# Sample value products of a hybrid decoder step: fp32 in pairs, or split into high and low parts row by row

## What is computed

```python
def attn_sample(q, k_new, v_new, iq, iw, ik_new, cache_k, cache_v, cache_ik, layer,
                page_table, rel_table):
    ...
    idx, valid = indexer_topk(iq, iw, ik_all, q_pos, topk)      # 256 of 1025 keys
    ...
    return sparse_attn(q, select(cache_k, k_new), select(cache_v, v_new), idx, q_pos,
                       valid, rel_table)

def sparse_attn(q, k_sel, v_sel, idx, q_pos, valid, rel_table):
    ...
    p = jax.nn.softmax(logits, axis=-1)
    out = jnp.einsum('btngk,btknd->btngd', p.astype(v_sel.dtype), v_sel)
```

## Time and profile before

| | us |
|---|---|
| median of three runs | 886.94 (886.18 to 889.48) |
| the profiled execution's own time | 886.94 |
| its span in the profile | 884.8 |
| PE busy | 847.3 |
| DVE busy | 581.1 |
| ACT busy | 427.4 |
| GpSimd (POOL) busy | 395.9 |
| sample value products, first and last start | 682.6 and 729.5 |

### The profile page before, as it was taken

One profiled execution on the slowest core, in us unless ns is written; L12 is line 12 of the kernel. 1 busy time (PEld: TensorE's weight loads), 2 busy tenths in 40 slices (PEclk: granted clock), 3 DMA queues, 4 the chain that ended last, 5 costly groups with the idle time before them and its releaser, 6 DMA issues.

```text
span 884.8 us, 18265 instructions
## 1 busy us (share of the span) xinstructions
PE 847.3 (96%) x6501; PEld 781.3 (88%) x6501; DVE 581.1 (66%) x1152; ACT 427.4 (48%) x1221; POOL 395.9 (45%) x575
## 2 busy tenths in 40 slices
PE   3999989999999999999999999898899999999998
PEld 3989979799999999999999999677688759998998
DVE  3536777899988998899956177866755337536111
ACT  5646573244455586584547366555534325422100
POOL 1443645219735583567662453287940205501310
PEclk9999999999999999999999999999899999999999
DMA  8212213101103120322033344833253544342422
GB/s 261 75 38 56 64 30 92 59 1 49 49 1 101 68 92 7 96 73 90 8 107 96 110 131 112 231 102 102 72 142 98 170 142 168 100 123 72 128 85 73
DMA packets 79422, 81.33 MB, mean 92 GB/s; under 512 B 20234, under 2 KB 68026, under 8 KB 79082
## 3 DMA queue, kind: packets, MB, share of 16 engines
q1 hardware_dynamic: 77722, 74.97, 28.3%
q0 software_dynamic: 1616, 5.25, 2.5%
HBM read 62.85 MB, written 17.34 MB: 91 GB/s over the span
## 4 chain that ended last, share of the span: by engine, by line
PE 57%; issue 14%; DMA 8%; DVE 7%; SPq 6%; POOL 4%; ACT 2%; DVEq 0%; POOLq 0%; ACTq 0%
PE psum L2116 16%; PE psum L1247 11%; PE psum L2113 7%; DMA index_keys_T<-in_cache_ikt,index_page_rows 6%; PE psum L1217 5%; SPq L565 4%; DVE flag L1899 3%; PE psum L2012 3%; SPq L556 3%; POOL w_low L514 2%; PE psum L1203 2%; PE psum L1996 2%; PE psum L1317 2%; PE psum L1182 2%; DVE bit_kept L1913 1%
## 5 line engine op out<-in xcount | busy, mean ns | idle before, releaser
L2116 PE MATMUL psum<-w_high,xT_high 128*128 128x256 f32 x720 | 204.2, 284 | 0.1
L2116 PE MATMUL psum<-w_low,xT_high 128*128 128x256 f32 x720 | 201.9, 280 | 0.0
L2116 PE MATMUL psum<-w_high,xT_low 128*128 128x256 f32 x720 | 201.6, 280 | 0.0
L1899 DVE TENSOR_SCALAR_CACHE_REDUCE flag<-scores,candidate 128x384 f16<-128x384 f32 (+2 forms) x192 | 181.7, 946 | 6.8
L514 POOL TENSOR_TENSOR w_low<-w_raw,w_high 128x256 fp32r<-128x256 f32 (+1 forms) x168 | 122.3, 763 | 78.8 <-ACT w_high L1576 69.4
L2116 PEld LDWEIGHTS psum<-w_high,xT_high 128*128 128x128 f32 x720 | 127.4, 177 | 2.6 <-ACT psum L1688 0.3
L2116 PEld LDWEIGHTS psum<-w_low,xT_high 128*128 128x128 f32 x720 | 127.6, 177 | 2.3
L2116 PEld LDWEIGHTS psum<-w_high,xT_low 128*128 128x128 f32 x720 | 127.4, 177 | 2.4
L2113 PE MATMUL psum<-xT_high,w_high 128*128 128x384 f32 (+3 forms) x312 | 102.1, 327 | 1.6 <-DVE xT_low L1826 1.2
L2113 PE MATMUL psum<-xT_high,w_low 128*128 128x384 f32 (+3 forms) x312 | 99.7, 320 | 0.0
L2113 PE MATMUL psum<-xT_low,w_high 128*128 128x384 f32 (+3 forms) x312 | 99.6, 319 | 0.0
(11 more groups left out here) (318 smaller groups left out, 1928.7 us busy)
## 6 DMA issues: line engine op xcount, KB each, us to landing
w_raw<-in_w_main SPq DMA_DIRECT2D x40, 512.0 KB, 3.9
page_keys<-in_cache_kt SPq DMA_DIRECT2D x64, 128.0 KB, 2.6
page_values<-in_cache_v SPq DMA_DIRECT2D x64, 128.0 KB, 2.2
x_rows<-in_x_prompt SPq DMA_DIRECT2D x8, 512.0 KB, 5.8
x_res<-in_x_prompt SPq DMA_DIRECT2D x32, 128.0 KB
out<-y_rows SPq DMA_DIRECT2D x32, 128.0 KB
hgate_spill<-stage SPq DMA_DIRECT2D x16, 128.0 KB
ho_spill<-ho_rows SPq DMA_DIRECT2D x4, 512.0 KB, 3.9
```

The lines of the kernel that those rows point to most:

```text
L1899: dve.tensor_scalar(JK[:, 0:w], sc, threshold(k), None, op, ALU.add, accum_out=CNT[:, k:k + 1]).then_inc(s["dve_chain"], 1)
L2116: last = pe.matmul(ps(BANK[n], w, rows(i)), x[:, k, row0(i):row0(i) + rows(i)], ww[:, sl, k, 0:w], start=first, stop=final)
```

## The change

The value products are made of split operands, and row by row:

- **Operands.** ACT copies each row's 128 x 2048 values to a rounded fp32r tile, page_values_high (two of them, a new job "values_high" two steps ahead of the products). DVE subtracts it from the values and writes page_values_low over the raw tile (a new job "values_low", one step ahead). prob_T is split into high and low as well, when it is copied out of PSUM.
- **Products.** For each page, one fp32r product with 40 stationary columns (8 high probabilities, 24 of other rows whose results are not read, 8 low probabilities) against the high values, and one with the 8 high probabilities against the low values. The product of the two low parts is left out. The new value's product stays fp32. Row b's job does all its pages, with outputs at partitions 0 and 32 of one half of the bank.
- **Outputs.** ACT copies the part at partition 32, and DVE adds the part at partition 0.
- **Buffers.** Three raw buffers take the place of five; the other two hold the high parts. SP loads rows 0 to 2 ahead, and rows 3 to 7 behind the mix loads, each when the products of row b-3 are done. The first output weights wait for seven rows of products and no longer for six.

```diff
-        VP = [over(W0 + o, (f"page_values_{x}", [NPG, UW], F32))[0]
-              for x, o in enumerate((-8192, 0, 16384, 8192, 24576))]
+        VP, VPL = ([over(W0 + o, (f"page_values{part}_{x}", [NPG, UW], dt))[0] for x, o in enumerate((-8192, 0, 16384))]
+                   for part, dt in (("", F32), ("_low", F32R)))
+        VPH = [over(W0 + o, (f"page_values_high_{x}", [NPG, UW], F32R))[0] for x, o in enumerate((8192, 24576))]
...
-        PTP, _e = over(S0 + SCW * 4, ("prob_T", [NPG, BR], F32))
+        PTP, _e = over(S0 + SCW * 4, ("prob_T", [NPG, 2, 2, 32], F32R))
...
-        for n in range(SB):
-            SIDE.setdefault(VALUES_AT[n], []).append(("values", n))
+        for b in range(SB):
+            SIDE.setdefault(VALUES_AT[b] - 2, []).insert(0, ("values_high", b))
+            side = SIDE.setdefault(VALUES_AT[b] - 1, [])
+            side.insert(0 if b > 0 else len(side), ("values_low", b))
+            SIDE.setdefault(VALUES_AT[b], []).append(("values", b))
...
-                x = b % 5
+                x = b % 3
...
-                elif b < 5:
-                    sp.wait_ge(s["sample_hgrn_ready"], 1)
-                    sp.wait_ge(s["sample_state_out"], 32)
                 else:
-                    sp.wait_ge(s["sample_values_done"], 2 if b < 7 else 4)
+                    sp.wait_ge(s["sample_values_done"], b - 2)
...
-            for b in range(5):
+            for b in range(3):
                 load_value_pages(b)
...
-            for b in range(5, SB):
+            for b in range(3, SB):
                 load_value_pages(b)
-            sp.wait_ge(s["sample_values_done"], SB - 2)
+            sp.wait_ge(s["sample_values_done"], SB - 1)
...
-            sp.wait_ge(s["sample_out_copied"], SB // 2)
+            sp.wait_ge(s["sample_out_copied"], 2 * SB)
...
-                elif kind == "values" and b % 2 == 1:
+                elif kind == "values":
                     act.wait_ge(s["sample_values_done"], b + 1)
-                    o = b // 2 % 2 * UW
-                    act.activation(OSM[0:SB, b - 1, :], ps(6, UW, AH, 0, o), ACT.Copy)
-                    act.activation(OSM[0:SB, b, :], ps(6, UW, 32 + AH, 32, o), ACT.Copy).then_inc(s["sample_out_copied"], 1)
+                    act.activation(OSM[0:SB, b, :], ps(6, UW, 32 + SB, 32, b % 2 * UW), ACT.Copy)\
+                        .then_inc(s["sample_out_copied"], 1)
+                elif kind == "values_high":
+                    act.wait_ge(s[f"value_pages_in{b % 3}"], 128 * (b // 3 + 1))
+                    if b < 2:
+                        act.wait_ge(s["sample_hgrn_ready"], 1)
+                        act.wait_ge(s["sample_state_out"], 32)
+                    else:
+                        act.wait_ge(s["sample_values_done"], b - 1)
+                    act.activation(VPH[b % 2][:, :, :], VP[b % 3][:, :, :], ACT.Copy).then_inc(s["sample_values_high"], 1)
...
-                    dve.tensor_copy(PTP[:, :, :].rearrange("p g n -> p (g n)"), ps(6)).then_inc(s["sample_probs_T_ready"], 1)
+                    high, low = PTP[:, :, :, 0, :], PTP[:, :, :, 1, :]
+                    probs = ps(6).rearrange("p (g a n) -> p g a n", g=NPG, a=2)
+                    link(dve.tensor_copy(high, probs))
+                    dve.tensor_tensor(low, probs, f(high), ALU.subtract).then_inc(s["sample_probs_T_ready"], 1)
...
+                elif kind == "values_low":
+                    dve.wait_ge(s["sample_values_high"], b + 1)
+                    dve.tensor_tensor(VPL[b % 3][:, :, :], VP[b % 3][:, :, :], f(VPH[b % 2][:, :, :]), ALU.subtract)\
+                        .then_inc(s["sample_values_low"], 1)
+                elif kind == "values":
+
+                    dve.wait_ge(s["sample_out_copied"], 2 * b + 1)
+                    dve.tensor_tensor(OSM[0:SB, b, :], OSM[0:SB, b, :], ps(6, UW, SB, o=b % 2 * UW), ALU.add)\
+                        .then_inc(s["sample_out_copied"], 1)
...
+                    pe.wait_ge(s["sample_values_low"], b + 1)
...
+                    ge(pe, s["sample_out_copied"], 2 * b)
+                    both, first = ps(6, UW, 32 + AH, o=b % 2 * UW), ps(6, UW, AH, o=b % 2 * UW)
+                    probs = PTP[:, :, :, :, :].rearrange("p g a k n -> p (g a k n)")
+                    for g in range(NPG):
+                        o = 128 * g + 64 * (b // 4) + AH * (b % 4)
+                        if g == NPG - 1:
+                            pe.matmul(first, PN[0:SB, AH * b:AH * (b + 1)], VN[0:SB, :], start=False, stop=False)
+                            pe.matmul(first, probs[:, o:o + AH], VPL[b % 3][:, g, :], start=False, stop=False)
+                        last = pe.matmul(both, probs[:, o:o + 32 + AH], VPH[b % 2][:, g, :], start=g == 0, stop=g == NPG - 1)
+                        if g < NPG - 1:
+                            pe.matmul(first, probs[:, o:o + AH], VPL[b % 3][:, g, :], start=False, stop=False)
```

More of the change, by code:

```diff
@@ L1226, in mix @@
                 if x == 0:
-                    pe.wait_ge(s["sample_out_copied"], SB // 2)
+                    pe.wait_ge(s["sample_out_copied"], 2 * SB)
                 for h in range(2):
@@ L1303, in sample @@
                 elif kind == "values":
-                    pair, half = b // 2, b % 2
-                    first = 2 * pair
-                    if half == 0:
-                        for x in (first, first + 1):
-                            pe.wait_ge(s[f"value_pages_in{x % 5}"], 128 * (x // 5 + 1))
-                        ge(pe, s["sample_out_copied"], pair - 1)
+                    pe.wait_ge(s["sample_values_low"], b + 1)
                     if b == 0:
@@ L1312, in sample @@
                         pe.wait_ge(s["new_prob_ready"], 1)
-                    out_ = [ps(6, UW, 32 * x + AH, 32 * x, pair % 2 * UW) for x in range(2)]
-                    for g in range(4 * half, 4 * half + 4):
-                        for x in range(2):
-                            h = slice(AH * (first + x), AH * (first + x + 1))
-                            last = pe.matmul(out_[x], PTP[:, g, h], VP[(first + x) % 5][:, g, :], start=g == 0, stop=False)
-                    if half == 1:
-                        for x in range(2):
-                            h = slice(AH * (first + x), AH * (first + x + 1))
-                            last = pe.matmul(out_[x], PN[0:SB, h], VN[0:SB, :], start=False, stop=True)
+                    ge(pe, s["sample_out_copied"], 2 * b)
[9 more added lines that the diff above has]
+                            pe.matmul(first, probs[:, o:o + AH], VPL[b % 3][:, g, :], start=False, stop=False)
                     last.then_inc(s["sample_values_done"], 1)
```

## The result

The changed kernel takes 891.1 us (median of 20 runs), the kernel before 883.9 us (20 runs). The ratio is 1.0068, 95% interval 1.0048 to 1.0089: slower by 4 to 8 us, where 5.7 us were forecast (892.6 against 886.94, the median of the first three runs, which lay 3.0 us above that of the twenty). The profiled execution spans 887.0 us. PE is as busy as before, 96%; ACT and DVE have the conversions on top.

The account below looks back on a forecast made before the run. PE, busy 96%, was taken as the bound, waiting on SP's page loads: row 7 lands at 726.7, conversions end 731.5, first mix 737.6 instead of 732.02. So 886.94 + 5.6, with tenths 892.6 us; range 888.0 to 896.0.

Parts of the forecast that it names:

- S: Stretch from the first value product to the first mix transpose, 49.25 us in the kernel before; 5.6 us more forecast.
- The hole before and its cause: Attention loop, after step 33's transposes: PE idle 2.11 us plus 1.52 at low clock, 3.6 us, ended by SP's pace.
- Late rows set the end: Page loads on SP: row 3 first issued at 685.3, periods of 8.8; row 7 lands at 726.7, 4.8 us later.
- Behind the landing: After row 7's pages land at 726.7: conversions and add until 731.5, then DVE's branch to the first mix at 737.6.
- PE's products: Value products: sixteen fp32r records 1.89 us plus new-value product 0.43 per row; eight rows 18.6 us, 1.8 lost while warm.
- Conversions of rows 0 to 6 hidden: ACT copies and DVE subtractions for these rows cost nothing, hidden under PE's scores, attention values and transposes.
- PE's idle time ahead of row 7: Before the last values group: 4 us or more, in two pieces, ended by ACT's exp and DVE's subtraction.
- B: Rival: the same chain with SP never held up, 4.2 us lost, 891.0 us; chance 0.22.
- A: Main case: the sum over late pages and the chain behind row 7's landing, 892.6 us; chance 0.60.
- C: Rival: pages come in time, only PE's own work counts, 20.4 becomes 18.6 us, time 885.1; chance 0.07.
- D: Rival: SP held up in each period, or low clock twice: about 8.5 us, 895.4; chance 0.08.
- E: Rival: split products run at the 0.215 step, not 0.118; 1.6 us more per row, 899 or above; chance 0.03.

Follow-up runs that it names:

- experiment 3: Kernel before, with fixed page numbers in place of the page table's, so no register loads per row: ratio 0.9963 to the kernel before, S = 45.63 us.
- experiment 4: Kernel before, with the loads of mix 0 and 1 issued by GpSimd instead of SP: 882.65 us against 884.96, ratio 0.9967, S = 45.63 us.
- experiment 1: Kernel before, with only rows 3 and 4 loaded behind the mix loads; products, buffers and engines' work unchanged: ratio 1.0057, S = 54.74 us.
- second look: The same changed kernel profiled once more, nothing edited: S = 55.85 us and one time of 892.71 us.
- Experiment 6: Changed kernel with DVE's first two mix_rows at steps 28 and 31 instead of 33: ratio 1.0102 to the kernel before, S = 53.06 us.
- experiment 2: Changed kernel with fixed page numbers in place of the page table's, so no register loads per row: ratio 0.9999 to the kernel before, S = 48.59 us.
- experiment 7: Changed kernel with ACT writing each row's high part twice: ratio 1.0117, S = 61.19 us.
- experiment 8: Changed kernel with mix loads and pages of rows 4 and 6 fetched by GpSimd, first two mix_rows at steps 28 and 31: ratio 1.006, S = 52.62 us.
- experiment 9: Changed kernel with GpSimd's four gating products held back until row 2's high part is there, no DMA on GpSimd: S = 55.59 us in one execution.
- experiment 10: Like experiment 8, but GpSimd makes its four gating products before fetching row 4's pages: ratio 0.999, S = 49.04 us.

## Why the prediction was right

The direction, the size and the mechanism held: S grew by 5.1 and 6.6 us in two profiles where 5.6 were forecast. That the time itself came within 1.5 us of 892.6 is in part luck: the base of 886.94 was 3.0 us above the median of twenty runs, and the loss was somewhat above the sum (7.2 us between the medians). Point by point:

- **The hole before and its cause.** 3.6 us, from SP's pace: shown twice, by taking the register loads away (experiment 3) and by taking the mix loads off SP (experiment 4), with S = 45.63 in both.
- **Late rows set the end.** Shown by experiment 1, in which they alone cost 0.57%. Row 3 first issued 2.6 us behind the first value product in the forecast, 2.9 and 3.9 measured; periods 8.8 in the forecast, 8.82 and 8.98 in the mean; row 7's landing 6.2 us behind its first issue, 6.0 and 5.8 measured.
- **Behind the landing.** Landing to DVE's add: 4.8 us forecast, 4.6 measured. Landing to mix: 10.9 forecast, 10.2 and 10.3 measured. DVE's branch with the two mix_rows ended last in the first profile, as said; in the second look PE's did, the two nearly level. Experiment 6 took the mix_rows away, and PE's branch ended last.
- **PE's products.** Sixteen fp32r records at 0.118 us: right. The new-value product was taken at 0.43 us; its two records stand in the chain with 0.52. A row's job lasts 2.5 us (711.31 to 713.84 in experiment 2), not 2.3, of which the step behind it gives a little back, and the change's own cost with early pages is 3.0 us (experiments 2 and 3), 2.4 of them PE's, and not 1.8. This term was mis-sized, and it did not reach the time because the pages were later still.
- **Conversions of rows 0 to 6 hidden.** Right in the sum; PE's idle time for a low part is 0.37 us once. But experiment 7 shows that there was less room than the busy shares of the earlier trace rows suggested: an average over 46 us says nothing of who waits behind a conversion at one place.
- **PE's idle time ahead of row 7, four us in two pieces: wrong.** There was one of 1.69 us ahead of row 6, and the low clock that followed it used up the rest. It came from ACT's wait for row 6's pages, which the forecast had taken for a small loss, and the forecast let the clock fall only at row 7. The sum did not hang on it, since the pages' chain passes beside PE.
- **Rivals.** B (SP never held up) gave 891.0 and so fits the measured time as well as A does; it is out by its mechanism, as the second period is 9.59 us, then 10.23, and by S, which it lets grow by 4.2. What holds SP up there was not settled: one of its issues takes 1.0 and 1.6 us instead of 0.33. C was the wrong sign; experiments 2 and 3 close it, since even with early pages the change costs 3.0 us. D did not come: both profiles of the changed kernel have one long period and not four. E is out, the records run at 0.118.

What the forecast did not have at all is the exclusion of DVE and GpSimd. It is in the changed kernel too, off the chain: in the first profile a product of GpSimd took 1.96 us at 681.94, behind the subtraction that had begun at 680.48; in the second look a product took 3.32 and a subtraction 3.27.

## What to carry to other kernels

Before splitting an fp32 product into reduced-precision ones, see whether the old ones already run two at a time: the step between records in the timeline tells it (0.114 us a record here, 0.222 one by one), and the split then gained nothing here. Fewer buffers move transfers behind other work in the same queue; count that queue's own time for an item, register loads included (here 8.6 to 10 us a row, against some 6 us from one row's products to the next), since it goes on setting the pace long after the wait for the buffer has been met. Before moving work onto an idle engine, look at what the neighbour does in the same moment: an engine that is free in the busy table may still block another.

## What the runs showed of the hardware

**VectorE and GpSimd exclude each other.** While both work on two float32 operands in SBUF, whichever comes second waits for the whole instruction of the other: 2.29 became 6.20, 3.41 and 3.27 us for the subtraction, 1.27 became 1.96, 3.34 and 3.32 for the product. The one that waits is not always next: in experiment 8 three further products went ahead of it. The Trainium skill (SBUF — State Buffer, section "SBUF: two separate sides") states this as an exclusive lock on a port pair, taken by a VectorE operation with two SBUF inputs against a GpSimd operation that reads SBUF; the trace agrees in experiment 9 to within 0.2 us. GpSimd's DMA issues left the subtraction at 2.29 us (experiment 10).

**The clock fell after short idle times.** PE idle for 1.39 us (experiment 1, at 706.7) kept the full clock: the group behind it took 1.90 us. Idle for 1.69 us in the changed kernel (up to 720.24), it had a granted clock of 0.50 from 722 us on; in experiment 7, after 0.97 and 1.20 us of idle time around one group of transposes (up to 712.37), it had 0.50 from 713 us on.

**A page that is found through a table costs SP's queue time of its own.** Each page takes SP one register load (0.27 us busy, one every 0.55 us) and one issue every 0.52 us, so 8.55 us per row of eight; with fixed page numbers rows 5 and 6 lie 3.7 us apart (experiment 3, the kernel before).
